# Thirty-two prompt tokens leave the dense first expert product of a PEER layer for gathered rows

## What is computed

```python
def peer_ffn(xn, w_q, sub_keys, u, v):
    q = (xf @ w_q).reshape(n, PEER_HEADS, 2, PEER_DK // 2)
    s = jnp.einsum('nhpd,hpkd->nhpk', q, sub_keys).astype(jnp.float32)
    sv, si = lax.top_k(s, PEER_TOPK)
    cand = (sv[:, :, 0, :, None] + sv[:, :, 1, None, :]).reshape(n, PEER_HEADS, PEER_TOPK * PEER_TOPK)
    ...
    tv, tsel = lax.top_k(cand, PEER_TOPK)
    g = jax.nn.softmax(tv, axis=-1).reshape(n, PEER_HEADS * PEER_TOPK).astype(xn.dtype)
    ...
        act = jax.nn.gelu(jnp.einsum('nd,ned->ne', xt, u[it]), approximate=False) * gt
        return jnp.einsum('ne,ned->nd', act, v[it])
```

## Time and profile before

| | us |
|---|---|
| median of three runs | 2133.39 |
| the three runs | 2134.4, 2125.04, 2133.39 |
| the profiled execution | 2121.02 |
| its span | 2119.2 |
| PE busy | 2048.2 (97%) |
| VectorE busy | 1527.9 (72%) |
| ScalarE busy | 860.5 (41%) |
| GpSimd busy | 607.6 (29%) |

### The profile page before, as it was taken

One profiled execution on the slowest core, in us unless ns is written; L12 is line 12 of the kernel. 1 busy time (PEld: TensorE's weight loads), 2 busy tenths in 40 slices (PEclk: granted clock), 3 DMA queues, 4 the chain that ended last, 5 costly groups with the idle time before them and its releaser, 6 DMA issues.

```text
span 2119.2 us, 29889 instructions
## 1 busy us (share of the span) xinstructions
PE 2048.2 (97%) x11176; PEld 1775.2 (84%) x11176; DVE 1527.9 (72%) x2689; ACT 860.5 (41%) x900; POOL 607.6 (29%) x436
## 2 busy tenths in 40 slices
PE   7999998998799999999999999989999999999997
PEld 6987776997799888888888888878888888888886
DVE  5988745555534988988899985767767777677765
ACT  4330145333333454445454445433334433344343
POOL 2010010221300015677576767001211212222200
PEclk9999999999899999999999999999999999999999
DMA  5564492443344666666666666788888888988974
GB/s 203 170 189 139 154 357 81 168 150 108 110 140 145 213 214 213 205 221 205 221 206 211 215 221 226 278 318 327 332 345 334 320 333 341 355 335 335 364 247 141
DMA packets 89309, 497.67 MB, mean 235 GB/s; under 512 B 16672, under 2 KB 16816, under 8 KB 35920
## 3 DMA queue, kind: packets, MB, share of 16 engines
q1 hardware_dynamic: 65904, 406.83, 53.9%
q0 software_dynamic: 18672, 72.87, 9.4%
q10 hardware_dynamic: 4656, 17.04, 2.1%
HBM read 457.78 MB, written 38.13 MB: 234 GB/s over the span
## 4 chain that ended last, share of the span: by engine, by line
PE 86%; DMA 5%; DVE 4%; ACT 3%; issue 1%; POOL 0%; SPq 0%; DVEq 0%; ACTq 0%; POOLq 0%
PE acc L1309 21%; PE mis L1545 14%; PE acc L1545 14%; PE acc L1310 11%; PE acc L1290 6%; PE acc L1291 5%; PE acc L1292 5%; PE acc L1335 4%; DMA raw<-in_v 4%; PE acc L1429 2%; DVE wl L754 2%; ACT wh L468 1%; PE mis L1404 1%; PE mis L1380 1%; DMA gin<-G 1%
## 5 line engine op out<-in xcount | busy, mean ns | idle before, releaser
L754 DVE TENSOR_TENSOR wl<-raw,wh 128x2048 fp32r<-128x2048 f32 x310 | 709.1, 2289 | 314.3 <-ACT wh L468 309.1
L468 ACT ACTIVATE wh<-raw 128x2048 fp32r<-128x2048 f32 x310 | 592.8, 1913 | 423.0 <-DMA raw<-in_v 394.4
L1309 PE MATMUL acc<-xhl,wh 128*128 128x512 f32 x2048 | 713.9, 392 | 2.0 <-DVE wl L754 2.0
L1310 PE MATMUL acc<-xhl,wl 128*128 128x256 f32 x2048 | 575.5, 281 | 0.0
L1671 POOL DMA_INDIRECT G<-gsum,cell x256 | 369.6, 1444 | 395.9 <-DVE same L1125 321.0
L1309 PEld LDWEIGHTS acc<-xhl,wh 128*128 128x128 f32 x2048 | 384.1, 188 | 88.3 <-DVE wl L754 2.3
L1310 PEld LDWEIGHTS acc<-xhl,wl 128*128 128x128 f32 x2048 | 386.4, 189 | 0.0
L1290 PE MATMUL acc<-xhl,wh 128*128 128x288 f32 x768 | 231.6, 302 | 25.4 <-DVE wl L790 14.0
L1291 PE MATMUL acc<-xhl,wh 128*128 128x288 f32 x768 | 228.9, 298 | 0.0
L1292 PE MATMUL acc<-xhl,wl 128*128 128x288 f32 x768 | 228.0, 297 | 0.0
L659 ACT ACTIVATE hsum<-acc 128x256 f32<-128x256 f32 x128 | 49.2, 384 | 342.1 <-PE acc L1310 323.5
(11 more groups left out here) (266 smaller groups left out, 2524.5 us busy)
## 6 DMA issues: line engine op xcount, KB each, us to landing
raw<-in_u SPq DMA_DIRECT2D x128, 1024.0 KB
raw<-in_v SPq DMA_DIRECT2D x128, 1024.0 KB
raw<-in_w_mix SPq DMA_DIRECT2D x28, 1024.0 KB
G<-zero SPq DMA_DIRECT2D x16, 1024.0 KB, 14.0
raw<-in_w_out SPq DMA_DIRECT2D x16, 1024.0 KB
raw<-in_w_pq SPq DMA_DIRECT2D x16, 1024.0 KB
h<-hbg ACTq DMA_DIRECT2D x32, 512.0 KB
hin<-h SPq DMA_DIRECT2D x32, 512.0 KB, 7.5
```

Of the source, the lines that this page charges most:

```text
L468: act.activation(wh[:, n % 4], raw[:, n % 4], ACT.Copy).then_inc(hi_done, 1)
L754: dve.tensor_tensor(wl[:, n % 4], raw[:, n % 4], wh[:, n % 4].bitcast(F32), ALU.subtract).then_inc(lo_done, 1)
L1309: pe.matmul(acc[:, s, :].rearrange("p (a n) -> p a n", a=2), wh[:, s, j, :], xhl[:, :, j, 0:NU], start=(j == 0), stop=False)
L1310: ins = pe.matmul(acc[:, s, 0:NU], wl[:, s, j, :], xh[:, j, 0:NU], start=False, stop=(j == DT - 1))
```

## The change

**32 tokens leave the dense U.** `NU` goes from 256 to 224: tokens 224 to 255 (partitions 96 to 127 of the second token half) take no part in the U product. Its matmuls have 448 and 224 columns. Their 32 x 128 picked experts are handled as the samples' are: `own_pick` on GpSimd gathers 32 times 1 MB of rows of U, `own_dot` on VectorE makes 32 dot products with `xrow_a`, ACT applies GELU in eight small pieces, and `own_hidden` on GpSimd scatters 32 x 128 values into a zeroed array `h_own` in DRAM, of which each load for V brings 128 KB more (`hin_a`). V still covers all 256 tokens.

**The operand is normalised first.** GpSimd makes `xn` = h x reciprocal norm in four instructions in PQ, and `normal_hi` (ACT) and `normal_lo` (VectorE) split it in 16 pieces each at PQ's last slot; the first U slot waits for each piece. So the evacuation of U needs no multiply, and takes two slots at a time: one ACT copy and one VectorE add of 2 x 224 columns, 64 times each.

**Routing starts in PQ.** Nine of the 36 routing parts and two gate steps run in PQ. Two copies of each unit are gone and the pairs of 256-element operations are single ones of 512. Gates and cells are made two heads of one token half at a time, the half with the 32 tokens first.

**Sums and writes.** The first head of each half has no earlier head, and its gates are written to G as they are; 224 sums are left, 16 of them in PQ. GpSimd writes from PQ on, with the 32 gathers among its 256 writes of G (`A_PICKS`), and the 32 `own_hidden` writes behind some heads.

**Rows of PE.** `turn_rows` runs twice: for the 32 tokens after U slot 2, for the samples after slot 115. The last query scores are taken behind the first U slot.

**V.** All 32 sample dots are in V (slots 0 to 62), the adds at slots 65 + 13n/8; the product of `hin` and `gin` is two instructions; for the first block it comes at U slot 126, with ACT's split at slot 127 and VectorE's after the U loop.

```diff
-NU = NP_
+NA = 32
+NU = NP_ - NA
...
-V_ADDS = {V_GELU + 1 + 15 * n // 8: n for n in range(PICKS)}
+DOT_SLOTS = list(range(10, 71, 4)) + [78, 82, 86, 90] + list(range(92, 116, 2))
+A_DOTS = {n: g for g, n in enumerate(DOT_SLOTS)}
...
+V_DOTS = {2 * n: n for n in range(PICKS)}
+V_GELU = 2 * PICKS
+V_ADDS = {V_GELU + 1 + 13 * n // 8: n for n in range(PICKS)}
...
-            def u_evac(it, s):
-                slot_ready(U0, it, s)
-                if s == 0:
-                    dve.wait_ge(gelu_done, it + 1)
...
-                dve.tensor_tensor(hadd[:, s % 2, :], acc[:, s, 0:NU], hsum[:, s % 2, :], ALU.add).then_inc(acc_free, 1)
-                dve.wait_ge(acc_free, slot_no(U0, it, s) + 5)
-                dve.tensor_tensor(hbg[:, s, :], hadd[:, s % 2, :], rstd[:, 1, 0:NU], ALU.mult).then_inc(scaled, 1)
+            def u_evac(q):
+
+                slot_ready(U0, 0, 2 * q + 1)
+                if q % 2 == 0:
+                    dve.wait_ge(gelu_done, q // 2 + 1)
+                dve.wait_ge(half_out, q + 1)
+                c = 2 * (q % 2)
+                dve.tensor_tensor(hbg[:, c:c + 2, :], acc[:, c:c + 2, 0:NU], hsum[:, q % 2], ALU.add).then_inc(acc_free, 2)
...
+            def own_dot(g):
+
                 if g == 0:
                     dve.wait_ge(xrow_out, 4)
+                dve.wait_ge(pick_a_in[g % 2], 16 * (g // 2 + 1))
+                rows = ring_a[g % 2]
+                dve.tensor_tensor_reduce(rows[:], rows[:], xrow_a[:], 1.0, 0.0, ALU.mult, ALU.add, hs_a[:, 0, g:g + 1]).then_inc(dot_a_done, 1)
...
                 for j in range(DT):
-                    pe.matmul(acc[:, s, :].rearrange("p (a n) -> p a n", a=2), wh[:, s, j, :], xhl[:, :, j, 0:NU], start=(j == 0), stop=False)
+                    if first:
+                        pe.wait_ge(split_lo, 3 * DT + CT + j + 1)
+                    pe.matmul(acc[:, s, 0:2 * NU].rearrange("p (a n) -> p a n", a=2), wh[:, s, j, :], xhl[:, :, j, 0:NU], start=(j == 0), stop=False)
                     ins = pe.matmul(acc[:, s, 0:NU], wl[:, s, j, :], xh[:, j, 0:NU], start=False, stop=(j == DT - 1))
...
+            def own_pick(g):
+
+                a, r = g // K16, g % K16
+                if g == 0:
+                    pool.wait_ge(pq_score, 16)
+                    pool.wait_ge(xrow_turned, 1)
+                if r == 0:
+                    pool.wait_ge(packed_in, 16 * GROUP * (a + 1))
+                if g >= 2:
+                    pool.wait_ge(dot_a_done, g - 1)
+                pool.indirect_dma_start(ring_a[g % 2][:], None, dr["ur"],
+                                        bass.IndirectOffsetOnAxis(ap=packed[:, 0, a, r:r + 1], axis=0)).then_inc(pick_a_in[g % 2], 16)
```

More of the change, by code:

```diff
@@ L1012, in pq, with normal_lo @@
                     dve.tensor_tensor(qp[:, s % 2, :], acc[:, s, 0:N], rstd[:, 1, :], ALU.mult).then_inc(acc_free, 1)
-            for i in range(4):
-                pq(i, i == 0)
+                    first_heads(4 * i + s)
+            def normal_lo():
+                for j in range(DT):
+                    split(xl[:, j, 0:NU], xn[:, j, 0:NU], par[:, Q_GFFN + j:Q_GFFN + j + 1], xh[:, j, 0:NU], 3 * DT + CT + j + 1)
             iota16 = iota[:, 0:K16]
@@ L1023, in route @@
             def route(un, part):
-                S = [sun[:, j, :] for j in range(2)]
+                S = [stok[:, un, j, :] for j in range(2)]
                 if part == 0:
-                    waited(0)
-                    own.done(dve.tensor_copy(sun[:], stok[:, ds(un, 1), :, :].rearrange("p a j c -> p (a j) c")))
                     waited(0)
@@ L1054, in route @@
                         waited(0)
-                own.done(dve.tensor_copy(one(tv[:, ds(un, 1), :]), top[:]))
                 own.done(dve.tensor_scalar(tab[:, 0, :], tsel[:], 4, None, ALU.logical_shift_right))
                 own.done(dve.tensor_scalar(tab[:, 1, :], tsel[:], 15, None, ALU.bitwise_and))
-                for j in range(2):
-                    waited(1)
-                    own.done(dve.tensor_tensor(eqb[:, j], bcast(tab[:, j, :], K16, 2), bcast(iota16, K16, 1), ALU.is_equal))
@@ L1061, in route @@
[L1061 to L1078 removed]
+                waited(0)
@@ new lines, in route @@
+                own.done(dve.tensor_tensor(eqb[:], bcast(tab[:], K16, 3), bcast(bcast(iota16, K16, 1), 2, 1), ALU.is_equal))
+                waited(0)
+                own.done(dve.tensor_tensor(eqb[:], eqb[:], bcast(i12f[:], K16, 2), ALU.mult))
+                waited(0)
+                own.done(dve.tensor_reduce(gij[:, 1:3, un, :], eqb[:], AX.X, ALU.add))
+            def u_evac(q):
[3 more added lines that the diff above has]
+                dve.wait_ge(half_out, q + 1)
+                c = 2 * (q % 2)
+                dve.tensor_tensor(hbg[:, c:c + 2, :], acc[:, c:c + 2, 0:NU], hsum[:, q % 2], ALU.add).then_inc(acc_free, 2)
@@ L1107, in head_cells @@
                 own.done(dve.tensor_copy(blk[:], j_))
-                for t in range(2):
-                    own.done(dve.tensor_scalar(cellf[:, t, :], i_[:, t, :], float(BLK * NU), cst[:, C_TOK + t:C_TOK + t + 1], ALU.mult, ALU.add))
-                own.wait(2)
+                own.done(dve.tensor_scalar(cellf[:], i_, float(BLK * NP_), cst[:, C_TOK + t:C_TOK + t + 1], ALU.mult, ALU.add))
+                own.wait(1)
                 own.done(dve.tensor_scalar(blk[:], blk[:], 3, None, ALU.logical_shift_right))
@@ new lines, in gate_sum @@
+            def gate_sum(m):
+                (t, h), r = SUM_UNITS[m // K16], m % K16
+                if r == 0:
+                    own.wait(0)
+                if m >= 2:
+                    dve.wait_ge(sums_ready, m - 1)
+                u = HEADS * (1 - t)
+                dve.scalar_tensor_tensor(same[:, m % 2, 0:h + 1, :], expert[:, t, 0:h + 1, :], expert[:, t, h, r:r + 1], gij[:, 0, u:u + h + 1, :],
+                                         ALU.is_equal, ALU.mult, accum_out=gsum[:, t, h, r:r + 1]).then_inc(sums_ready, 1)
@@ new lines, in _, with sums, first_heads @@
+            summed = 0
+            def sums(count):
+                nonlocal summed
+                for _ in range(count):
+                    gate_sum(summed)
+                    summed += 1
+            def first_heads(m):
+                if m in PQ_PARTS:
+                    un, part = PQ_PARTS[m]
+                    if part == 0:
+                        dve.wait_ge(pq_out, 2 * (un % HEADS) + 2)
+                    route(un, part)
+                if m in PQ_TOP:
+                    softmax_top(PQ_TOP[m])
+                if m in PQ_GATES:
+                    gates_and_cells(PQ_GATES[m])
+                sums(PQ_SUMS.get(m, 0))
@@ L1282, in _, with product @@
         def _(pe):
-            def product(out, w, mh, ml, n, before=None):
+            def product(out, w, mh, ml, n, before=None, freed=None):
                 wr, blocks = w
@@ L1476, in pq @@
                 for s in range(4):
-                    slot(PQ0, i, s, xh, xl)
+                    slot(PQ0, i, s, xh, xl, freed=xn_free if i == 3 and s == 3 else None)
                     if first and s == 0:
@@ L1647, in _ @@
             pool.wait_ge(slot_used, PQ0)
-            pool.wait_ge(const_in, 16)
+            pool.wait_ge(rstd_done, 4)
+            for a in range(4):
+                pool.tensor_tensor(xn[:, 4 * a:4 * a + 4, :], hT[:, 4 * a:4 * a + 4, 0:NP_], bcast(rstd[:, 1, 0:NP_], 4, 1), ALU.mult).then_inc(xn_ready, 1)
             def pick(g):
```

442 lines of the change are left out of this document (269 added, 173 removed).

## The result

The changed kernel takes 2105.84 us (median of four runs, 2097.56 to 2109.44), the kernel before 2133.89 (four runs, 2125.04 to 2136.48): a ratio of 0.9878, 95% interval 0.9856 to 0.9899. In a later group of runs it was 2108.8 against 2128.4, 0.9915 (0.9899 to 0.9931). So the gain is 20 to 28 us, where 60 were forecast. The direction was right, the size less than half.

The account below looks back on a forecast made before the run. PE's matmuls in U were taken as the bound: 2121.0 - 81 + 3.6 + 2 + 8 + 4.5 + 3 = 2061.1 us on the profiled execution, carried to the median as 2073 us, range 2052 to 2106.

Parts of the forecast that it names:

- the price of the first turn of rows: PE in U: the turn of rows runs a second time, 3.57 us, entered as +3.6 us.
- a slow mode for 224 columns: Rival: split matmuls of 224 columns run like unsplit float32, 0.39 us each, +580 us, about 2650; chance 0.04.
- I take -81, since 288, 256 and 512 columns lie on one line.: PE in U: 96 fewer columns a pair at 0.41 ns, over 2048 pairs, save 81 us.
- The rival with a floor under the short matmul: U: the short matmul stays at 0.12 us, -54 instead of -81 (2100); chance 0.11 together with late loads.
- late loads: Rival in U: raw tiles late behind gathers, up to 15 us (2088); chance 0.11 together with the floor.
- no row below 256 columns: Argument for the floor rival: the profile rows show no split matmul of under 256 columns.
- Bounds 0 to 21 us; I take +8: GpSimd in U: a late gather delays a dot, which holds the `wl` behind it, and PE: +8 us.
- the first rival: GpSimd too slow: dots block it or heads come late, some 30 us instead of 8, 2095 to 2112; chance 0.18.
- No cost taken: Loads in U: raw tiles beside the added gathers stop PE for nothing; 0 to 15 us kept as bounds.
- +2 for it (0 to 8): U: VectorE's fixed order at slots 38, 42 and 90, and the first slot's wait for splits, cost PE 2 us.
- +3 (0 to 8): V: 32 dots, not 26, and denser adds whose gathers share the DMA engines lengthen it by 3 us.
- Entry to V: V's first accumulation: later product and low split, and the first block's load, make PE wait +4.5 us (1 to 9).

Follow-up runs that it names:

- the second trace: The changed kernel run once more, unchanged, as the measure for a later group: 2108.8 us, 0.9915 of the kernel before.

## Why the prediction was wrong

What bounds the kernel was read rightly, PE's matmuls in U, and the price of the first turn of rows (3.5 us), the entry and the absence of a slow mode for 224 columns came as said. These steps failed:

- **"I take -81, since 288, 256 and 512 columns lie on one line."** The term is the largest mistake of size. From 0.348 to 0.316 us a pair is 0.032 x 2048 = 66 us, not 81; with the spread of the distances (mean 0.3485 to 0.3174) 64. The line ended at about 240 columns, one step below the last point that I had. The rival with a floor under the short matmul had a price of -54 and was given, together with late loads, 0.11; "no row below 256 columns" overlooked the 0.112 us of the turn's records.
- **"Bounds 0 to 21 us; I take +8"** for GpSimd. The mechanism of the first rival happened: dots block GpSimd, gathers come late, VectorE waits 13.7 us for them and holds the next `wl`, and the chain goes through GpSimd's list for 69 us. But it is not the whole: gathers and writes cost 14 us in U (11 by the second trace), and of these some 4 are a raw tile beside the samples' gathers, for which the sum had "No cost taken". The evidence that I weighed against it (adds and gate sums don't block) was about another instruction, and decided nothing for a dot.
- **"+2 for it (0 to 8)"** for VectorE's fixed order. The dots alone cost 9.6 us of U: some 2 at slots 34 to 44, near two of the three slots that I had named (38, 42 and 90), but also 3.6 at 98 and 101, and 3 at the second turn, since the samples' rows stand behind the last dot. Their sum of busy time was right (forecast 551 us, 557.9 in the window above), which again says little of the waits. All gaps of U together are 32.9 us, where 7.3 + 13.6 were due.
- **"+3 (0 to 8)"** for V. It was 8 to 15 in the two traces. I had not priced the small load of `hin_a`, which stands in the same queue ahead of the tile that the chain goes through, some 3 to 5 us, and I had priced the adds' gathers, every 1.6 slots, too low: without the gathers of V's rows the gaps of 6 to 11 us behind 1750 us are gone. The "6 us" that PE stopped in V before was itself a reading of busy time; by its starts it is 13.9.
- **Entry to V**, +4.5 forecast, +5.2 and +6.7 measured. It was right by its bounds, but not by its reason alone: the product itself came late. VectorE at the entry after, beside the earlier trace rows:

```profile
1360.85 2.29 DVE L844 TENSOR_TENSOR wl<-raw,wh 128x2048 fp32r<-128x2048 f32 x1 [5.60 <-ACT wh L512]
1363.06 2.02 DVE L1308 TENSOR_TENSOR gin<-hin,gin 128x1792 f32<-128x1792 f32 x1
...
1368.46 2.28 DVE L1313 TENSOR_TENSOR al<-gin,ah 128x2048 fp32r<-128x2048 f32 x1
```

`wl` of the slot ahead had waited 5.60 us for `wh`, whose load stood behind the block's, and the product stands behind `wl`; then the split of ACT, the evacuation and the low split follow one another up to 1370.74.

On the measured medians the forecast fell short by 32 to 40 us: 17 from the pair, 8 to 12 from U's gaps, 5 to 12 from V and up to 2 from the entry. The base, a trace 8 to 12 us under its own median, did no harm, since the sum was carried over to the median.

## What to carry to other kernels

When matmuls get shorter, compare the shortest one with the least distance of two weight loads that the trace shows (here 0.11 us, in a turn of rows) before pricing columns by a line; the last columns may be free already. Work that moves off the busiest engine onto engines in fixed order costs by where it stands, not by its sum of busy time, and a gather that is issued late can cost twice, on the engine that waits for it and on the load that it then runs beside. Where a run removes two things at once, look in the traces at which waits went. A stage whose loads already end on the chain (here V, 12.26 us a tile) has no free place even for a small transfer.

## What the runs showed of the hardware

- A pair of split matmuls, one of L columns and one of S, with weights of their own, repeats every 0.417 (L + S) + 28 ns, but not below 0.417 L + 129 ns (316 ns for 448 and 224 and for 448 and 192 columns, 289 for 384 and 192; 348 for 512 and 256, the one size on the first form), with the short one's weight load 0.11 us behind the long one's. All at the 2.4 GHz level, clock 1.00 in the window of U.
- A VectorE dot product of 128 x 2048 with a running sum holds up an indirect DMA's issue on GpSimd until 0.83 us behind its end (29 issues in the changed kernel's trace), as a tensor_tensor of that size does (157); an issue that began 0.04 us ahead of the dot took its usual 0.96 us.
- A raw tile of 1 MB beside two gathers of 1 MB took 10.04 us from issue to landing (changed kernel, 1307.44).
